# Moving five pre norms' column sums into the tile behind them, and feeding the last three squares of two post norms straight to TensorE

## The reference

```python
def rms_norm(x, g):
    y = x * lax.rsqrt(jnp.mean(x * x, axis=-1, keepdims=True) + EPS)
    return y * g

# first block
h = x
z  = rms_norm(h, g_mix_pre) @ w_in            # head "1"
mix = ... @ w_out
h = h + rms_norm(mix, g_mix_post)             # post norm "p1"
ff = square(relu(rms_norm(h, g_mlp_pre) @ w_up)) @ w_down     # head "2"
h = h + rms_norm(ff, g_mlp_post)              # post norm "p2"
gate = sigmoid(rms_norm(h, g_ple_pre) @ w_ple_gate)           # head "3"
h = h + rms_norm((p @ w_ple_proj) * gate, g_ple_post)         # post norm "p3"
# second block
z = rmsnorm(h, ln_mix_g) @ w_in_2             # head "4": gated attention and linear attention
h = h + merged @ w_out_2
a, u = split(rmsnorm(h, ln_ffn_g) @ w_ffn_in_2)               # head "5"
h = h + (silu(causal_dwconv(a)) * u) @ w_ffn_out_2
```

## Time and profile before

| | |
|---|---|
| median of 3 runs | 1515.39 us (1513.42 to 1517.8) |
| the profiled execution, its own time | 1511.38 us |
| its span | 1509.6 us |
| TensorE busy | 1455.1 us, 96% of the span |
| VectorE, ScalarE, GpSimd busy | 54%, 38%, 17% |
| mean granted clock of TensorE | 0.992 of full speed |
| mean DMA rate | 86 GB/s |

### The profile page before, as it was taken

The page is one execution under the profiler, slowest core; times in us unless marked ns, Lnnn a source line. Parts: engine busy times, 40 slices in busy tenths (PEclk is TensorE's granted clock), DMA queues, the critical chain, the costliest instruction groups (busy, mean ns, idle before and its releaser), DMA issues.

```text
span 1509.6 us, 17723 instructions
## 1 busy us (share of the span) xinstructions
PE 1455.1 (96%) x6972; PEld 1187.7 (79%) x6972; DVE 818.1 (54%) x1150; ACT 571.0 (38%) x836; POOL 257.7 (17%) x169
## 2 busy tenths in 40 slices
PE   7999999999999999889999999999999999999998
PEld 6776768888888887766789877788887888888887
DVE  4598566433333347674767753634444665534554
ACT  4344534522323224443364565422224443323310
POOL 4144244300101013340034202200003000000000
PEclk9999999999999999998999999999999999999999
DMA  6221222332333332211211111232332233232331
GB/s 225 70 71 56 70 71 84 98 100 96 98 98 98 98 98 74 81 56 56 71 56 52 34 56 43 89 107 86 100 106 86 70 112 103 93 111 85 98 98 70
DMA packets 35987, 129.18 MB, mean 86 GB/s; under 512 B 4008, under 2 KB 4136, under 8 KB 35904
## 3 DMA queue, kind: packets, MB, share of 16 engines
q1 hardware_dynamic: 35904, 128.04, 27.4%
HBM read 125.91 MB, written 2.10 MB: 85 GB/s over the span
## 4 chain that ended last, share of the span: by engine, by line
PE 84%; DVE 7%; ACT 3%; POOL 3%; issue 2%; DMA 0%; SPq 0%; POOLq 0%; DVEq 0%; ACTq 0%
PE P L1013 24%; PE P L1015 24%; PE P L1014 24%; PE P L1244 2%; PE P L1034 1%; PE P L1035 1%; PE P L1036 1%; DVE P L1785 1%; POOL AC L2262 1%; ACT WH L1324 1%; DVE WL L1630 1%; POOL H L2271 1%; POOL DD L2262 0%; PE P L1227 0%; PE P L1130 0%
## 5 line engine op out<-in xcount | busy, mean ns | idle before, releaser
L1013 PE MATMUL P<-AH,WH 128*128 128x512 f32 x1104 | 445.3, 403 | 25.8 <-DVE AL L1635 12.5
L1015 PE MATMUL P<-AH,WL 128*128 128x512 f32 x1104 | 433.8, 393 | 0.0
L1014 PE MATMUL P<-AL,WH 128*128 128x512 f32 x1104 | 433.6, 393 | 0.0
L1324 ACT ACTIVATE WH<-WR 128x1024 fp32r<-128x1024 f32 x233 | 245.0, 1052 | 335.1 <-PE P L1015 323.3
L1630 DVE TENSOR_TENSOR WL<-WR,WH 128x1024 fp32r<-128x1024 f32 x216 | 273.0, 1264 | 169.7 <-ACT WH L1324 169.3
L1013 PEld LDWEIGHTS P<-AH,WH 128*128 128x128 f32 x1104 | 209.6, 190 | 77.3 <-issue 27.0
L1015 PEld LDWEIGHTS P<-AH,WL 128*128 128x128 f32 x1104 | 209.4, 190 | 44.8
L1014 PEld LDWEIGHTS P<-AL,WH 128*128 128x128 f32 x1104 | 209.9, 190 | 41.9 <-issue 0.7
L1013 PE MATMUL P<-FH,WH 128*128 128x512 f32 x432 | 168.0, 389 | 0.0
L1014 PE MATMUL P<-FL,WH 128*128 128x512 f32 x432 | 168.0, 389 | 0.0
L1015 PE MATMUL P<-FH,WL 128*128 128x512 f32 x432 | 168.0, 389 | 0.0
(11 more groups left out here) (301 smaller groups left out, 1858.2 us busy)
## 6 DMA issues: line engine op xcount, KB each, us to landing
WR<-in_ws SPq DMA_DIRECT2D x233, 512.0 KB, 3.6
out<-Y SPq DMA_DIRECT2D x8, 256.0 KB, 2.0
H<-in_xT SPq DMA_DIRECT2D x3, 512.0 KB, 8.6
C<-in_const SPq DMA_DIRECT2D x1, 946.5 KB, 11.0
H<-in_xT SPq DMA_DIRECT2D x2, 256.0 KB, 4.6
PR<-in_pT SPq DMA_DIRECT2D x1, 512.0 KB, 4.5
PM<-in_params SPq DMA_DIRECT2D x1, 121.5 KB, 2.9
GKU<-in_gku SPq DMA_DIRECT2D x1, 32.0 KB, 10.5
```

What stands on the lines that cost most here:

```text
L1013: e.matmul(P, wh, xh, start=start, stop=False)
L1014: e.matmul(P, wh, xl, start=False, stop=False)
L1015: ins = e.matmul(P, wl, xh, start=False, stop=stop)
L1324: e.activation(m.WH[:, c % NW, :], m.WR[:, c % NRAW, :], ACT.Copy).then_inc(*at.up("w_hi", "w_hi", c))
```

## The change

In `head` the sums step leaves its place before j = 7 and comes inside the last tile, before that tile's third block; the spread leaves its place before the last tile and comes before that tile's eighth block. In post norms "p1" and "p3" `direct` becomes 3: GpSimd adds blocks 1 to 4, and TensorE takes squares 5, 6 and 7 from SQ. After square 5 and after square 6 TensorE signals that the block is summed, which is what ScalarE waits for before it writes square 7 into the same place as square 5. Post norm "p2" keeps `direct` 1.

```diff
@@ head
         for j in range(8):
-            if j == 7:
-                self.sums(s, 0)
             for m, t in enumerate(got):
                 self.block(t, specs[m][j], (x, j), j == 0, j == 7)
             if j < 5:
                 make(j + 3)
             if j < 6:
                 rest(j + 2)
-        b = self.spread(s)
-        out = got + [self.tile(specs[len(got)], [(x, j) for j in range(8)])]
+        t = self.ring()
+        for j in range(8):
+            if j == 2:
+                self.sums(s, 0)
+            if j == 7:
+                b = self.spread(s)
+            self.block(t, specs[len(got)][j], (x, j), j == 0, j == 7)
         self.say("rbc", s, b)
-        return out
+        return got + [t]
@@ part (post norm p1), and likewise for p3
-                    self.say("square", "p1", m, 1)
+                    self.say("square", "p1", m, 3)
...
-        return self.post("p1", 1)
+        return self.post("p1", 3)
@@ sums (TensorE)
-        if direct:
-            w.wait_ge(*at("square", n, 7))
+        for i in range(8 - direct, 8):
+            w.wait_ge(*at("square", n, i))
             for q in range(4):
-                ins = e.matmul(P[:, q:q + 1], SQ[:, 1, 128 * q:128 * q + 128], one, start=False, stop=True,
+                ins = e.matmul(P[:, q:q + 1], SQ[:, i % 2, 128 * q:128 * q + 128], one, start=False, stop=i == 7,
                                skip_group_check=True)
+            if i < 7:
+                ins.then_inc(*at.up("summed_direct", "summed", n, i))
         ins.then_inc(*at.up("full", "full", t.id))
```

More of the change, by code:

```diff
@@ L500, in mlp1 @@
                 self.say("ple_gated", m - 1)
-                self.say("square", "p3", m - 1, 1)
+                self.say("square", "p3", m - 1, 3)
         for m in (6, 7):
             self.say("ple_gated", m)
-            self.say("square", "p3", m, 1)
-        return self.post("p3", 1)
+            self.say("square", "p3", m, 3)
+        return self.post("p3", 3)
     def mixer2(self, ready):
```

## The result

The changed kernel takes 1519.73 us (median of 19 runs, 1515.19 to 1522.84) against 1513.28 us before (19 runs, 1510.16 to 1517.8). The ratio is 1.0039, 95% interval 1.0028 to 1.0049: 5.9 us slower (4.2 to 7.4). Forecast were +5.0 us.

A forecast was written before the change was run, and what follows sets the result against it. TensorE, busy 96% of the span, was taken as the bound. Terms 2.5+1.25-3.15+1.0+1.9+1.1+0.4 gave +5.0 us, so 1515.39+5.0 = 1520.4 us; range 1518 to 1522.5 for this case, 1513.2 to 1525 overall.

The forecast's parts named there:

- RBC's lateness: Last tile of each head: RBC can start 0.42 us before the tile's end and is done 0.26 us after it.
- behind head 1: Token tiles wait for two banks that RBC's readers free: +1.8 and +0.7 us, sum +2.5.
- the chunks behind head 5: Weight chunks behind RBC come late, +1.4 then +1.9 us; the largest counts, so +1.9 in all.
- Head 2: Last tile ends 0.45 us later and a weight chunk is wanted 0.80 us before it is ready: sum +1.25 us.
- The AL wait: Head 2, before block j = 7: with the sums gone, TensorE waits 1.3 us for AL.
- Head 3: The 3.37 us wait for GpSimd goes, and slow clock behind it: -3.15 us, of which some 1.7 is clock.
- p1: Post norm: two more groups of sums add 1.78 us, the 0.67 us wait for GpSimd goes: +1.1 us.
- the bounds: Effects the trace doesn't show, left out of the sum; for the clock during p1's one-column matmuls, 0 to +1.8 us.
- p3: Post norm: the same added 1.78 us of sums less the 1.38 us wait for GpSimd: +0.4 us.
- Rival B: Not slower, since readers of RBC don't hold TensorE: -2.2 us, 1513.2, within 0.3%; chance 0.12.
- Rival A: More clock: half speed behind head 1 and in p1 and p3, two such places: +8.4 us, 1523.8; chance 0.2.
- The carry from head 3 through p3: Head 3 being earlier carries over p3, as ScalarE's and VectorE's work there hangs on RBC, 2.3 us earlier.

The follow-up runs named there:

- the kernel of the last experiment: The whole change with GpSimd's square of RBC and the split of the second input (ple_in) said eight tiles later; ratio to before 1.0031 (1.0015 to 1.0048).
- the early kernel: The whole change, but sums at the first block of the last tile and spread at the fifth; ratio to before 0.999 (0.9977 to 1.0004), -1.5 us.
- the heads alone: Five heads as in the change, post norms with direct 1 as before; ratio to before 1.0031 (1.0019 to 1.0044), +4.7 us.

## Why the prediction was right

**RBC's lateness.** The step that carries the prediction is "RBC can start 0.42 us before the end of the tile". Behind head 5 the spread starts at 1179.65, RBC at 1180.29, and the last matmul of the tile at 1180.55:

```profile
1179.65 0.60 PE L1097 MATMUL P<-C,NR 128*128 128x128 f32 x4
...
1180.55 0.40 PE L1018 MATMUL P<-AH,WL 128*128 128x512 f32 x1
```

One matmul's 0.23 behind it, at 1180.78, the next tile would start. So spread and block took 1.13 us (1.12 forecast), the copy followed the spread's start by 0.64 (0.70), and RBC started 0.49 before the tile's end. From start to start the next tile was 1.79 and 0.56 late behind head 1 (forecast 1.8 and 0.7), 0.98 behind head 3, 0.97 behind head 4 and 1.07 behind head 5 (forecast 1.0 each), and the chunks behind head 5 brought it to +2.06 (+1.9).

**Head 2** came out 0.4 us higher. The AL wait was forecast (1.3, measured 1.27), but the last tile ends 0.67 later and not 0.45, and the chunk costs 0.97 from start to start and not 0.80.

**Head 3** saved 2.90 of 3.15, the clock behind the 3.37 us wait included: the stretch from 616 to 622 us is at 1.00 after, and at 0.76 before.

**p1** is the term that was mis-sized most: +1.75 for +1.1. Up to the end of the sums it is +1.22, of which 0.3 is that the sums already ran in part at the lower level (0.90 in the window above; at 1.00, in the kernel of the last experiment, the 24 records take 2.86 us and not 3.17). Behind the sums it is +0.53: there the clock stands at 0.50 over 3.4 us. The sum had clock in p1 at nothing and named it only among the bounds (0 to +1.8). In four profiled executions direct 3 with three warm matmuls took 15.25, 14.41, 14.09 and 14.08 us, always with the clock down behind the sums (0.78 and 0.79 over 8 us in the last two); direct 1 took 13.50 to 13.52 in four and 12.63 and 12.65 in two, where it was not.

**p3** is +0.67 for +0.4, and again the difference is clock: up to the end of the sums it is +0.19, behind them +0.48, at a clock of 0.78 where it was 1.00 before. The square of block 7 was covered as forecast.

So the waits were right in place and size, and what the sum lacked, 1.7 us by the stages, is mostly the clock in p1 and p3 and head 2's 0.4. That the median fell within 0.7 us of the forecast 1520.4 is partly luck: the kernel before measured 1513.28 us in the comparison, 2.1 less than the 1515.39 that the forecast was added to, and the difference came out larger than +5.0; the two nearly cancel.

**Rival B**, readers of RBC that don't hold TensorE, fell with the waits above, and with the early kernel, in which they go. **Rival A**, more clock, was true for parts of p1 and p3, together some 1.3 us and not the two places of 1.7; behind head 1 it did not come. The carry from head 3 through p3 was right with direct 3 and would have been wrong without it, as the heads alone showed.

## What to carry to other kernels

A wait that the profile shows at one instruction may be cheaper than its cure: before a producer is moved later, follow its result to the readers that free a buffer, and further to whatever their engine does behind them (here weight chunks four tiles on). Move only the case that waits, as far as it needs; here that was one head of five, and the version with that head alone was the only one whose measured intervals lay wholly below the kernel before. Adding work to the engine that bounds the kernel, to spare one that is 17% busy, paid here only where that work filled a wait that was really there.

## What the runs showed of the hardware

The same kernel, with only head 3 moved, was profiled twice. In the first execution p3 took 13.32 us and p1 13.52, in the second 15.03 and 12.63, with the same instructions and the same waits (1.32 and 1.30 us in p3). The difference is the granted clock. First execution, stretches of p3 and p1:

```profile
646.80:654.20 7.40, 4.36 (x14) 1.75 (x13) 5.82 (x16) 1.24 (x2) 1.26 (x1) 1.00 0.00 0
...
218.00:221.90 3.90, 3.90 (x10) 1.74 (x10) 1.97 (x12) 0.00 (x0) 0.00 (x0) 0.56 0.00 0
```

Second execution:

```profile
646.40:655.20 8.80, 7.18 (x13) 3.15 (x13) 5.81 (x16) 1.26 (x2) 1.26 (x1) 0.65 0.00 0
...
217.40:220.40 3.00, 2.39 (x10) 1.09 (x10) 1.96 (x12) 0.00 (x0) 0.00 (x0) 1.00 0.00 0
```

So a place with idle time or one-column matmuls ahead of it drops to 1.2 GHz in one execution and not in the next. From 139 to 146 us, where no kernel here differs, the clock is 1.00 before and 0.64 in the second execution above, and the stretch between head 1 and p1 takes 144.5 or 147.4 us accordingly. Runs of one kernel differ by up to 8 us, and the clock goes with it: of the kernel before, the four runs at a mean clock of 0.987 took 1516.7 us on average and the three at 0.992 took 1510.7 (same chip). Which places make up the difference in a run without a profile is not shown. One profile can't tell a change of 4 us by its span; stages can, where the clock of the stage is read with them.
